# Opening of a two-block transformer kernel: norm by halves, rotary angles behind both token tiles, gate input products split around two weight tiles, and one tile left out of a ring count

## The reference

```python
def reference(x, p, positions, ...):
    x = first_block(...)      # 2 hybrid layers
    return second_block(x, mem_2, ...)

def first_block(...):
    x = layer_norm(x, ln_in_g, ln_in_b)
    for i in range(DEPTH):
        x = hybrid_layer(x, p[i], positions, w_in[i], ...)

def hybrid_layer(x, p_i, positions, w_in, ...):
    h = x @ w_in                                    # 1024 x 1704
    qa, ka, va, qb, kb, vb, qi, ki, wi = split(h)
    qa, ka, qb, kb, qi = rope(each, positions)      # angles = positions * inv
    ki = rope(layer_norm(ki, idx_k_g, idx_k_b), positions)
    ...
    ple = (p_i @ w_pp) * sigmoid(x @ w_pg)
    return layer_norm(ALPHA * x + ffn + ple, ln2_g, ln2_b)
```

## Time and profile before

| | us |
|---|---|
| median of 3 runs | 1554.95 |
| lowest, highest | 1549.97, 1555.04 |
| span of the profiled execution | 1552.6 |
| PE busy in it | 1497.1 (96%) |
| DVE busy | 1062.8 (68%) |
| ACT busy | 778.0 (50%) |

### The profile page before, as it was taken

The page is one execution under the profiler, slowest core; times in us unless marked ns, Lnnn a source line. Parts: engine busy times, 40 slices in busy tenths (PEclk is TensorE's granted clock), DMA queues, the critical chain, the costliest instruction groups (busy, mean ns, idle before and its releaser), DMA issues.

```text
span 1552.6 us, 21682 instructions
## 1 busy us (share of the span) xinstructions
PE 1497.1 (96%) x8433; PEld 1264.8 (81%) x8433; DVE 1062.8 (68%) x1713; ACT 778.0 (50%) x1162; POOL 123.2 (8%) x98
## 2 busy tenths in 40 slices
PE   8999999999899999999999999999999999999997
PEld 5877888888677888878877988888788779888886
DVE  7777587667766787676345566878863555677777
ACT  4563544444554444434565344666545653446563
POOL 0130000000210000011022000000010320000000
PEclk9999999999999999999999999999999999999999
DMA  7534655656235655644614745556536147345551
GB/s 260 196 101 138 217 190 190 212 172 209 93 119 172 235 190 190 226 157 135 193 56 152 252 134 172 185 190 216 176 121 195 54 151 257 126 168 184 189 190 66
DMA packets 184429, 265.03 MB, mean 171 GB/s; under 512 B 7368, under 2 KB 139398, under 8 KB 184200
## 3 DMA queue, kind: packets, MB, share of 16 engines
q1 hardware_dynamic: 178712, 258.38, 50.2%
q10 hardware_dynamic: 5616, 5.26, 1.0%
HBM read 258.38 MB, written 5.24 MB: 170 GB/s over the span
## 4 chain that ended last, share of the span: by engine, by line
PE 77%; DVE 13%; ACT 4%; issue 3%; DVEq 2%; POOL 1%; ACTq 0%; POOLq 0%; DMA 0%; SPq 0%
PE psw L815 18%; PE psw L814 8%; PE psw L742 8%; PE psw L744 7%; PE psw L743 7%; DVE wlo L1735 5%; PE psa L742 4%; PE psa L744 4%; PE psa L743 4%; PE psa L876 3%; PE psa L874 3%; PE psa L926 2%; PE psw L898 2%; PE psa L943 1%; PE psw L818 1%
## 5 line engine op out<-in xcount | busy, mean ns | idle before, releaser
L1735 DVE TENSOR_TENSOR wlo<-raw,whi 128x2048 fp32r<-128x2048 f32 (+3 forms) x199 | 449.9, 2266 | 124.5 <-ACT whi L1347 124.1
L815 PE MATMUL psw<-xboth,whi 128*128 128x512 f32 x1344 | 464.7, 396 | 1.2 <-DVE wlo L1735 1.2
L1347 ACT ACTIVATE whi<-raw 128x2048 fp32r<-128x2048 f32 (+3 forms) x199 | 375.0, 1885 | 175.6 <-PE psw L744 91.3
L814 PE MATMUL psw<-xboth,wlo 128*128 128x256 f32 x1176 | 327.9, 279 | 0.0
L815 PEld LDWEIGHTS psw<-xboth,whi 128*128 128x128 f32 x1344 | 242.7, 188 | 49.1 <-DVE wlo L1735 2.3
L814 PEld LDWEIGHTS psw<-xboth,wlo 128*128 128x128 f32 x1176 | 221.7, 189 | 7.5
L742 PE MATMUL psw<-whi,xboth 128*128 128x512 f32 (+3 forms) x472 | 181.8, 385 | 6.4 <-DVE wlo L1735 5.3
L744 PE MATMUL psw<-whi,xboth 128*128 128x512 f32 (+3 forms) x472 | 178.8, 379 | 0.0
L743 PE MATMUL psw<-wlo,xboth 128*128 128x512 f32 (+3 forms) x472 | 178.6, 378 | 0.0
L1409 ACT ACTIVATE r<-psw 128x512 f32<-128x512 f32 x88 | 52.5, 596 | 174.7 <-PE psw L815 164.2
L742 PE MATMUL psa<-whi,rr 128*128 128x512 f32 x352 | 137.5, 391 | 1.4 <-DVE rr L2365 1.3
(11 more groups left out here) (290 smaller groups left out, 2209.9 us busy)
## 6 DMA issues: line engine op xcount, KB each, us to landing
raw<-in_w_gu SPq DMA_DIRECT2D x44, 1024.0 KB, 5.1
raw<-in_ffn_w_up SPq DMA_DIRECT2D x42, 1024.0 KB, 5.1
raw<-in_w_down SPq DMA_DIRECT2D x22, 1024.0 KB, 4.9
raw<-in_ffn_w_down SPq DMA_DIRECT2D x22, 1024.0 KB, 4.8
raw<-in_w_in SPq DMA_DIRECT2D x20, 1024.0 KB, 5.3
raw<-in_xa_wkv SPq DMA_DIRECT2D x16, 1024.0 KB, 5.4
raw<-in_w_o SPq DMA_DIRECT2D x8, 1024.0 KB, 5.2
raw<-in_w_out SPq DMA_DIRECT2D x8, 1024.0 KB, 5.2
```

Source lines behind the costliest of these rows:

```text
L814: pe.matmul(bank[:, 0:S], wl[:, k, cols], xhi[:, k, :], start=False, stop=False)
L815: ins = pe.matmul(bank.rearrange("p (i s) -> p i s", i=2), wh[:, k, cols], xboth[:, :, k, :], start=k == 0, stop=k == KD - 1)
L1347: nc.scalar.activation(tile_flat("hi", i), tile_flat("raw", i), ACT.Copy).then_inc(hi_ready, 1)
L1735: v.tensor_tensor(tile_flat("lo", i), tile_flat("raw", i), tile_flat("hi", i).bitcast(F32), ALU.subtract).then_inc(lo_ready, 1)
```

## The change

Four edits, all in the opening of layer 0 of the first block:

- `norm` of token tile 0 waits for the two gain copies (`gb_ready` 2) ahead of L1762, and then for one bias copy ahead of each half of L1769, in place of all four copies at once.
- On DVE `angles` goes from behind the norm of token tile 0 to behind `turned_lo` of token tile 1; the statistics of the memory go ahead of `tables`. On ACT the Sin goes from behind the high part of q0 to behind `turned_hi` of token tile 1.
- On PE the gate input products of token tile 1 of layer 0 go behind passes (0,0) and (1,0), ahead of the transposes of token tile 1. On ACT the high part of q1 goes ahead of the copies of the gate inputs, that of q2 ahead of those of token tile 1. For layer 1 the order is as before.
- Tile 0 is left out of `split_ring`. That ring gives `hi_room`; with tile 0 in it the high part of q2 waited for `tile_done` 1, without it it waits for nothing. The values for all later tiles are the same, and so are the places in memory.

```diff
--- before.py
+++ after.py
@@ -238,7 +238,7 @@
     halved = [i for i in ring if tiles[i][0][1] not in ("w1", "kv", "pp")]
     hseq = {i: q for q, i in enumerate(halved)}
     split_order = []
-    split_ring = [i for i in ring if i not in between.values()]
+    split_ring = [i for i in ring if i not in between.values() and i != ti[(1, "pp", 0, 0)]]
     split_seq = {i: q for q, i in enumerate(split_ring)}
     for i in halved:
         here = [e for e in extra if extra[e] == i]
@@ -1012,9 +1012,7 @@
 
                 pe.wait_ge(*loaded(ti[(1, "pp", l, 0)]))
                 weight = tile_view("raw", ti[(1, "pp", l, 0)])
-                for t in range(NT):
-                    if t and l:
-                        norm_turns(x_in, 0)
+                def gate_input(t):
                     for half in range(2):
                         for kk in range(2):
                             tok = slice(t * P, (t + 1) * P)
@@ -1022,6 +1020,15 @@
                             ins = pe.matmul(psw[:, 2 * t + half, :], pT[l][:, kk, tok], weight[:, kk, col],
                                             start=kk == 0, stop=kk == 1)
                         ins.then_inc(tile_done if t and half else pp_part, 1)
+
+                def second_in_turns():
+                    if l == 0:
+                        gate_input(1)
+                    norm_turns(x_in, 1)
+                gate_input(0)
+                if l:
+                    norm_turns(x_in, 0)
+                    gate_input(1)
 
                 def head_turns(q):
 
@@ -1076,7 +1083,7 @@
                         pe.wait_ge(proj_ready, 8 * l + 2 * (g - 2) + t + 1)
 
                 token_stage(1, "in", l, 7, x_in, 3, 0, bank_free,
-                            {(2, 0): lambda: norm_turns(x_in, 1), (3, 0): param_turns,
+                            {(2, 0): second_in_turns, (3, 0): param_turns,
                              (4, 0): memory_turns, (5, 0): first_heads,
                              (6, 0): first_scores})
                 pe.wait_ge(relu_done, NT * l + 1)
@@ -1478,8 +1485,8 @@
             p_out(0, 0)
             turned_hi((1, "in", 0), 0)
             split(1)
-            act.wait_ge(angles_ready, 1)
-            nc.scalar.activation(angs[:, 4:6, :], angs[:, 4:6, :], ACT.Sin).then_inc(sines_ready, 1)
+            split(2)
+            nxt[0] = 2
 
             for l in range(L):
                 x_in = (1, "in", 0) if l == 0 else (1, "2", l - 1)
@@ -1492,14 +1499,16 @@
                         nc.scalar.activation(ple[:, t, half * 512:(half + 1) * 512], psw[:, 2 * t + half, :],
                                              ACT.Copy).then_inc(pp_ready, 1)
                     if t == 0 and l == 0:
-                        split(2)
-                        nxt[0] = 2
+                        serve((1, "pp", l, 0))
                     elif t == 0:
                         turned_hi(x_in, 0)
                 serve((1, "pp", l, 0))
 
                 def second_tokens():
                     turned_hi(x_in, 1)
+                    if l == 0:
+                        act.wait_ge(angles_ready, 1)
+                        nc.scalar.activation(angs[:, 4:6, :], angs[:, 4:6, :], ACT.Sin).then_inc(sines_ready, 1)
 
                 def heads_out(q):
                     act.wait_ge(heads_turned, 8 * l + q + 1)
@@ -1756,7 +1765,7 @@
                 dve.drain()
                 v.tensor_scalar(vare[:, t:t + 1], meanvar[:, t, 1:2], LN_EPS, None, ALU.add).then_inc(ln_var, 1)
                 if t == 0 and nm["n"] == 0:
-                    dve.wait_ge(gb_ready, 2 * NT)
+                    dve.wait_ge(gb_ready, NT)
                 elif t == 0 and "loads" in nm:
                     dve.wait_ge(gb_loaded, 32 * nm["loads"])
                 v.scalar_tensor_tensor(out=x[:, t, :], in0=x[:, t, :], scalar=meanvar[:, t, 0:1],
@@ -1766,6 +1775,8 @@
                 dve.drain()
                 for half in range(2):
                     h = slice(half * 512, (half + 1) * 512)
+                    if t == 0 and nm["n"] == 0:
+                        dve.wait_ge(gb_ready, NT + half + 1)
                     ins = v.scalar_tensor_tensor(out=x[:, t, h], in0=x[:, t, h], scalar=rstd[:, t:t + 1],
                                                  in1=nm["place"][:, 1, h], op0=ALU.mult, op1=ALU.add)
                     if signal:
@@ -1990,7 +2001,6 @@
             dve.wait_ge(x_loaded[0], 16)
             half_stats(xtok, 0)
             norm((1, "in", 0), xtok, 0)
-            angles()
             turned_lo((1, "in", 0), 0)
             split(1)
             dve.wait_ge(x_loaded[1], 16)
@@ -2002,10 +2012,11 @@
                 serve((1, "pp", l, 0))
                 if l == 0:
                     turned_lo((1, "in", 0), 1)
-                    tables()
+                    angles()
                     dve.wait_ge(mem_loaded, 16 * NT)
                     for t in range(NT):
                         half_stats(memory, t)
+                    tables()
                     dve.drain()
                     for t in range(NT):
                         v.bn_aggr(meanvar[:, t, :], stats[:, t, 0:2, :])
```

## The result

The changed kernel takes 1558.44 us as the median of 20 runs (1553.94 to 1560.14), the kernel before 1554.57 (20 runs, 1549.46 to 1558.77). The ratio is 1.0029, with a 95% interval of 1.002 to 1.0039: slower by some 4.5 us where 0.9 were forecast (the two medians are 3.9 apart, the means 4.0). The profiled execution took 1558.28, its span is 1556.5 against 1552.6, so 3.9 us are to be found in the traces. (Run and span differ by 1.8.)

What follows compares the result with a forecast made beforehand. PE bounds the kernel, with 77% of the chain; in the opening only its lateness at (3,0) counts. 2.0 us won and 2.9 lost give +0.9, so 1554.95 becomes 1555.9 us, range 1550.0 to 1559.0.

Steps and rivals of the forecast that it cites:

- Part 1: Norm of token tile 0 by halves: done at 11.32 instead of 13.37, transposes ending at 12.95, 1.8 us won.
- Part 2: Gate input products around two token tiles: (0,0) from 18.15, (2,0) at 27.6 instead of 29.58, 2.0 us won there.
- as many at the lower level as before: First gate inputs: four of eight steps at TensorE's lower clock level, as before, so they end at 17.8.
- rival 3: Opening does not gain: gate inputs all at the lower level or q1 late, (0,0) near 19.9; +2.6 us, chance 0.08.
- All covered, q5 with the least room, about 5 us: SP's queue: later loads of q4, constants and q5 still land before they are wanted, q5 about 5 us before PE.
- Part 3: Tile 0 not counted in the ring: q2's high part no longer waits for tile_done 1, stays at about 20; costs nothing.
- Part 4: Angles behind both token tiles: DVE finishes q3's low part at 41.3, PE waits 2.9 us before (3,0).
- The sum of the hand-over, +0.9: Start of (3,0): 2.0 us won at (2,0), 2.9 lost before (3,0), so 41.3 against 40.41.
- I take 0.9 to the end: Behind (3,0): everything up to token tile 0's index sums follows PE, so 0.9 us stays to the end.
- Rival 2: PE's wait before (3,0) slows the clock for dense passes behind it: +2.6, up to +4.3 us; chance 0.24.
- price for a long fall, 3.4: Slow clock behind (3,0)'s wait, lasting as long as at 411: about 3.4 us lost, in place of 1.7.
- the dense products in front of the wait as the argument against: Before (3,0): dense products stand until 38, whereas at 411 PE had only small ones, speaking against a clock drop.

Runs made afterwards that it cites:

- pe_kept_busy: The changed kernel with three fp32 identity products put into PE's wait behind the parameter transposes, ahead of (3,0); ratio to the kernel before 1.0007.
- after_both_busy: pe_kept_busy with two fp32 identity products ahead of PE's wait in the attention stage of both layers of the first block; ratio to the kernel before 0.9993.
- short_angles: The changed kernel with two of three steps of the angles' range reduction left out, so its angles are coarse; ratio to the kernel before 1.0023.
- angles_only: The kernel before with only angles, Sin and tables moved as in the change; ratio to the kernel before 1.0037.
- before_again: The kernel before, unchanged, in another profiled execution; span 1553.0 us.
- angles_back: The changed kernel with angles, Sin and tables back in their old places; ratio to the kernel before 0.9999.
- q3_low_first: The changed kernel with DVE doing q3's low part ahead of the tables and the memory norm; ratio to the kernel before 1.0003.
- gate_ring_only: The kernel before with only the change's gate input order and ring count, halves and angles as before; ratio to the kernel before 1.0022.

## Why the prediction was wrong

**Part 1 (halves)** was right. The second half of L1769 (L1780 in the changed kernel) ends at 11.31 (11.32 said), the transposes at 12.65 (12.95). GpSimd's rstd took 1.49 beside L1771 (the old L1762), which cost nothing.

**Part 2 (gate inputs)** was nearly right on PE: (0,0) at 17.82 (18.15), (2,0) at 27.0, the end of the transposes (26.75 in the timeline, with the overlap; 27.6 said), so 2.6 us won there, not 2.0. It took "as many at the lower level as before", and that came true for a cause it doesn't name: the clock's first rise moved with PE, from 17.4, 18.2 and 18.6 in three executions of the kernel before to 14.9, 14.9 and 14.5 in three of the changed one. Had it stayed at 17.4, some 5.5 of the eight steps would have taken 0.86 in place of 2.6, and the four gate inputs would have ended about 1.2 us later (an estimate from these steps), most of rival 3. Part 2 was wrong on SP's queue. "All covered, q5 with the least room, about 5 us" looked only at PE's need of q5. It left out ACT's order, in which the parameter and the memory copies stand behind q5's high part. In the changed kernel PE is late already, so the 4.28 us that ACT stands there show only a little; alone this part puts the index sum 3.1 us back.

**Part 3 (ring)** was not measured apart.

**Part 4 (angles)**: the angles took 3.67 (3.68 said), statistics, tables and memory norm 6.31 (6.34), (3,0) started at 40.80 (41.3). The wait was 3.26 (2.9 said). The sum of the hand-over, +0.9, was 0.39 in the first pair of profiles and 0.6 by three executions of each. With the clock kept up (pe_kept_busy, after_both_busy) the index sum stands at 62.46 and 62.43, 0.9 behind the mean of the kernel before's three: so much of the forecast was sound.

**The step that failed** is the one behind that sum: "I take 0.9 to the end". A wait of PE of three us was counted at its length, and the slower clock behind it was put at nothing. Rival 2 named what happened and priced it at 1.7; it was 1.7 in the profiles (from (3,0) to the index sum 22.63 to 22.75 against 21.02 with the clock kept up), and some 2.7 by the means of pe_kept_busy and the changed kernel. Why the means give a us more, which their scatter may hold, stays open. Rival 2's price for a long fall, 3.4, stands in no row: falls of 6.8 us took 2.8 in the attention stage (20.45 for 17.65). Rival 2 was given 0.24, with the dense products in front of the wait as the argument against. They did not help: three profiled executions of three had the fall, and even the wait of 2.06 in short_angles had one.

The Trainium skill (TensorE: Matmul & The Clock Gate, "Why this matters for your kernels") asks that PE isn't left idle between bursts of matmuls, or it goes back to half the clock. The trace of the changed kernel agrees, with half the clock behind 3.26 us of waiting. The rule is put for gaps longer than the 2.06 of short_angles and the 2.54 of angles_only, so the fall behind the first goes beyond it and the second doesn't speak against it. But "by that rule the drop is sure" was too much: before_again had 3.00 us of waiting in the attention stage and no fall.

**What was missing** is the attention stage. Its wait of 3.0 us stood in the kernel before already, seen only in its shorter form of 1.43, since in that execution a fall at 72.0 had slowed the product ahead of it. The 1.6 us between the two profiles there are of the executions: the kernel before took 17.62 to 20.45 in that stage, the changed one 19.11 to 20.65. Part of the scatter of the times may be of the same kind, which isn't shown run by run: one kernel's runs spread over 4 to 10 us, and an estimate from the products' 1.4 to 3.0 us for a fall makes that a few falls more or less.

The parts don't add: means of -2.8 (halves), +5.3 (angles), +3.3 (gate inputs and ring) give +5.8, the whole change has +4.0. That the angles' wait hides the late copies, and that the halves' gain ends in the same wait, is read from the traces; no run sets the sum right.

## What to carry to other kernels

Ask of each engine that is made early what it will wait for next, and what stands in front of that on every other engine: work that fills a gap costs nothing where it is and its full length where it is moved to. Follow a delayed load past its own reader, to all that stands behind the reader's instruction. Count a wait of TensorE of two to three us as longer than it may be: here a fall of the clock behind it added 1.7 us or more, in some executions of such waits and not in others. A few products without use, put into a wait that can't be shortened, were worth 0.15% to 0.2%. And profile one kernel more than once before a difference of a us or two in a far stage is put down to the change.

## What was not expected of the hardware

- TensorE's granted clock went to half for 3.4 or 6.8 us behind waits of 2.06 (short_angles), 2.36 and 2.49 (ahead of (0,0) in angles_back and q3_low_first), 3.26 (three of three) and 3.0 to 3.2 us (20 of 25); it did not behind waits of 2.25, 2.39, 2.54 and 2.58 in one execution each (q3_low_first, gate_ring_only, angles_only, angles_back). Two or three products in the wait, 2.0 to 2.8 us of work, kept it up in all four profiled executions that had them.
- The first rise of the clock differs by a us between executions of one kernel (17.4, 18.2 and 18.6 us in the kernel before), and it follows the program: 17.4 to 18.8 in the six profiled executions without the halves, in which PE waits 1.8 us ahead of the first transposes, and 12.7 to 15.5 in the eleven with them. Where it came at 12.7 (angles_back and q3_low_first) the gate inputs ended early, PE waited 2.4 us before (0,0), and the clock fell again at 19.5.
- The GpSimd power instruction on 128 elements took 0.55 us with DVE idle and 1.49 beside DVE's L1771, ending 0.4 us behind it.
